# Ten inner chunks of two feed-forward layers are turned in 32 x 32 blocks on VectorE, and ScalarE's and VectorE's orders in the two input projections are changed

## The reference, cut to what matters

```
# block 1
h = rms_norm(x, mix_norm_g);  proj = h @ w_in          # 1024 -> 8708, then four kinds of attention
x = x + gated_mix(proj) @ w_out
h = rms_norm(x, mlp_norm_g)
x = x + square(relu(h @ w_up)) @ w_down                # inner width 4096
x = rms_norm(x, final_norm_g)
# block 2
h = rms_norm(x, norm1_g);     proj = h @ w_in2         # 1024 -> 2560: q, k, v and u
u -> (a, g);  c = a * sigmoid(g)                       # 512 channels
conv = silu(layer_norm(causal_conv31(c)))              # depthwise, 31 taps
x = x + concat(attention(q, k, v), conv) @ w_out2
h = rms_norm(x, norm2_g)
x = x + (silu(h @ w_gate) * (h @ w_up2)) @ w_down2     # inner width 2816
```

## Time and profile before

| | before |
|---|---|
| median of 3 runs | 799.73 us (799.54 to 800.09) |
| profiled execution | 797.38 us |
| its span, first to last instruction | 795.6 us |
| granted TensorE clock | 1.000 |
| busy: PE / PEld / DVE / ACT / POOL | 98% / 83% / 60% / 51% / 6% |

### The profile page before, as it was taken

One profiled execution on the slowest core, in us unless ns is written; L12 is line 12 of the kernel. 1 busy time (PEld: TensorE's weight loads), 2 busy tenths in 40 slices (PEclk: granted clock), 3 DMA queues, 4 the chain that ended last, 5 costly groups with the idle time before them and its releaser, 6 DMA issues.

```text
span 795.6 us, 9723 instructions
## 1 busy us (share of the span) xinstructions
PE 781.3 (98%) x3930; PEld 657.2 (83%) x3930; DVE 475.3 (60%) x623; ACT 406.9 (51%) x542; POOL 49.3 (6%) x38
## 2 busy tenths in 40 slices
PE   7999999999999999999999999999999999999998
PEld 5888899887888888888888887878988888888896
DVE  6654374764866877454444448699857554545443
ACT  6566365454656646555544455654565344343441
POOL 1000000000001410000000004022000000000000
PEclk9999999999999999999999999999999999999999
DMA  9843334433445366555656564845133755555341
GB/s 333 327 160 107 132 132 142 167 116 107 159 161 202 116 204 230 194 190 169 211 166 203 164 206 153 324 136 189 54 107 105 238 185 184 186 188 183 106 160 53
DMA packets 68508, 136.25 MB, mean 171 GB/s; under 512 B 2416, under 2 KB 7152, under 8 KB 67824
## 3 DMA queue, kind: packets, MB, share of 16 engines
q1 hardware_dynamic: 68320, 134.59, 49.7%
q10 hardware_dynamic: 144, 1.05, 0.4%
HBM read 134.43 MB, written 1.05 MB: 170 GB/s over the span
## 4 chain that ended last, share of the span: by engine, by line
PE 89%; DVE 7%; ACT 2%; DMA 1%; issue 1%; SPq 0%; ACTq 0%; DVEq 0%
PE b L592 19%; PE b L594 19%; PE b L593 19%; PE SS L592 4%; PE SS L594 4%; PE SS L593 4%; PE TT L561 4%; PE OO L592 2%; PE OO L594 2%; PE OO L593 2%; DVE wlo L1513 2%; DVE ca L1986 1%; PE b L737 1%; PE OO L911 1%; PE SS L680 1%; DMA raw<-in_w_in 1%
## 5 line engine op out<-in xcount | busy, mean ns | idle before, releaser
L1513 DVE TENSOR_TENSOR wlo<-raw,whi 128x2048 fp32r<-128x2048 f32 (+2 forms) x123 | 274.4, 2232 | 156.0 <-ACT whi L1081 155.8
L1081 ACT CAST whi<-raw 128x2048 fp32r<-128x2048 f32 (+2 forms) x123 | 227.5, 1851 | 126.3 <-PE b L594 83.3
L592 PE MATMUL b<-whi,Ahi 128*128 128x512 f32 (+2 forms) x552 | 216.4, 392 | 1.2 <-DVE Alo L1536 0.9
L594 PE MATMUL b<-whi,Alo 128*128 128x512 f32 (+2 forms) x552 | 209.2, 379 | 0.0
L593 PE MATMUL b<-wlo,Ahi 128*128 128x512 f32 (+2 forms) x552 | 208.7, 378 | 0.0
L592 PEld LDWEIGHTS b<-whi,Ahi 128*128 128x128 f32 x552 | 104.3, 189 | 20.4 <-DVE Alo L1536 1.7
L594 PEld LDWEIGHTS b<-whi,Alo 128*128 128x128 f32 x552 | 104.1, 189 | 20.1
L593 PEld LDWEIGHTS b<-wlo,Ahi 128*128 128x128 f32 x552 | 104.4, 189 | 17.5
L592 PE MATMUL b<-whi,Bhi 128*128 128x512 f32 x154 | 60.9, 395 | 0.0
L594 PE MATMUL b<-whi,Blo 128*128 128x512 f32 x154 | 60.0, 390 | 0.0
L593 PE MATMUL b<-wlo,Bhi 128*128 128x512 f32 x154 | 60.0, 390 | 0.0
(11 more groups left out here) (278 smaller groups left out, 1054.0 us busy)
## 6 DMA issues: line engine op xcount, KB each, us to landing
raw<-in_w_in SPq DMA_DIRECT2D x40, 1024.0 KB, 5.0
raw<-in_w_up SPq DMA_DIRECT2D x16, 1024.0 KB, 5.4
raw<-in_w_dn SPq DMA_DIRECT2D x16, 1024.0 KB, 4.9
raw<-in_w_d SPq DMA_DIRECT2D x11, 1024.0 KB, 4.9
raw<-in_w_g SPq DMA_DIRECT2D x10, 1024.0 KB, 4.9
raw<-in_w_u SPq DMA_DIRECT2D x10, 1024.0 KB, 5.1
raw<-in_w_out SPq DMA_DIRECT2D x8, 1024.0 KB, 4.9
raw<-in_w_br SPq DMA_DIRECT2D x4, 1024.0 KB, 4.9
```

Source lines behind the costliest of these rows:

```text
L592: e.matmul(dst, xh, H[:, kc, c0:ce], start=first and kc == krs[0], stop=False)
L594: ins = e.matmul(dst, xl, H[:, kc, c0:ce], start=False, stop=last and kc == krs[-1])
L1081: e.copy(whi[:, s, 0:m], raw[:, r, 0:m]).then_inc(s_hi, 1)
L1513: e.tensor_tensor(wlo[:, s, 0:m], raw[:, r, 0:m], whi[:, s, 0:m].bitcast(F32), ALU.subtract).then_inc(s_lo, 1)
```

## The change

**Turns.** The eight PE transposes of chunks 1 to 6 and 1 to 4 are gone. DVE turns the chunk instead, from `ust` to a new buffer `hT` in SBUF, in 16 instructions (`turn_part`): each takes 32 partitions x 256 elements and transposes its eight 32 x 32 blocks. Three quarters of them stand before the groups 1 to 3 of `dn j-1` (`d2 j-1`), the last quarter before the first group of the next chunk. ACT's `hhi` and DVE's `hlo` are made from `hT`, before the next chunk's second and third group.

**First projection, ACT.** `te` and `pc` (now `banks1`) and `evac` stand ahead of the split of each step, where they stood behind it.

**Second projection.** `ug` writes its second half of channels to `tg` with two instructions per token half in place of six; ACT (`ph`) copies it from there to `hp` and `odd` with six copies at steps 9 and 10. Two taps of the convolution move from step 12 to step 16.

```diff
-    bg[9] += [("ut", 1), ("ug", 1)]
+    bg[9] += [("ut", 1), ("ug", 1), ("ph", 0)]
+    bg[10] += [("ph", 1)]
-    for s, n in ((10, 7), (12, 2), (14, 3), (18, 2)):
+    for s, n in ((10, 7), (14, 3), (16, 2), (18, 2)):
         bg[s].append(("cv", n))
...
+        hT = sb("hT", [128, 2, 4, S], c=r4)
...
+    HV = {("H", j): i for i, j in enumerate(range(1, 7))}
+    HV.update({("G", j): 6 + i for i, j in enumerate(range(1, 5))})
...
-            if 0 < j < 7:
-                turn_h()
...
         for c in range(18):
             for q, (ui, t) in enumerate(order1(c)):
+                if q == 0 and c > 1:
+                    evac(c - 1, 1)
+                if q == 3 and c:
+                    evac(c, 0)
+                banks1(4 * c + q)
                 after("p1", c, ui, t)
...
-                if j == 1 and q == 1:
-                    hidden_hi(0)
+                if j and q == 1:
+                    hidden_hi(j - 1)
...
+        def ph(t):
+            w.wait_ge(s_ug, t + 1)
+            w.wait_ge(s_pad, 1)
+            u0 = 15 + 64 * t
+            for k in range(2):
+                u = tg[:, t, 128 * k:128 * k + 128].rearrange("p (u r) -> p r u", r=2)
+                for i, p in ((2 * k, 0), (2 * k + 1, 64)):
+                    e.copy(hp[p:p + 64, i, u0:u0 + 64], u[p:p + 64, 0, :])
+                ins = e.copy(odd[:, k, u0:u0 + 64], u[:, 1, :])
+            ins.then_inc(s_ph, 1)
...
+        def turn_part(key, m, landed_h):
+            k, j = key
+            w.wait_ge(*landed_h)
+            src = ust[:, j % 2, :, :].rearrange("p t (k c) -> p t k c", k=4)
+            dst = hT[:, j % 2, :, :].rearrange("p k (t q) -> p t k q", t=2)
+            for i in range(4):
+                ins = e.transpose(dst[32 * m:32 * m + 32, :, :, 32 * i:32 * i + 32],
+                                  src[32 * i:32 * i + 32, :, :, 32 * m:32 * m + 32])
+            if m == 3:
+                ins.then_inc(s_hv, 1)
...
+                if ("H", j - 1) in HV and q == 0:
+                    turn_part(("H", j - 1), 3, (s_up, 2 * j))
+                if j and q == 2:
+                    hidden_lo(j - 1)
...
+                    if ("H", j) in HV and k:
+                        turn_part(("H", j), k - 1, (s_up, 2 * j + 2))
...
-            u0 = 15 + 64 * t
-            for k in range(2):
-                a = src[:, 256 + 128 * k:384 + 128 * k].rearrange("p (u r) -> p r u", r=2)
-                g = ca[:, 2 + k, 128 * t:128 * t + 128].rearrange("p (u r) -> p r u", r=2)
-                bias = pcol("glu_b", 2 + k)
-                for i, p in ((2 * k, 0), (2 * k + 1, 64)):
-                    e.scalar_tensor_tensor(
-                        out=hp[p:p + 64, i, u0:u0 + 64], in0=a[p:p + 64, 0, :], scalar=bias[p:p + 64, :],
-                        in1=g[p:p + 64, 0, :], op0=ALU.add, op1=ALU.mult)
-                ins = e.scalar_tensor_tensor(out=odd[:, k, u0:u0 + 64], in0=a[:, 1, :], scalar=bias, in1=g[:, 1, :],
-                                             op0=ALU.add, op1=ALU.mult)
+            for k in range(2, 4):
+                ins = e.scalar_tensor_tensor(
+                    out=tg[:, t, 128 * k - 256:128 * k - 128], in0=src[:, 128 * k:128 * k + 128],
+                    scalar=pcol("glu_b", k), in1=ca[:, k, 128 * t:128 * t + 128], op0=ALU.add, op1=ALU.mult)
```

More of the change, by code:

```diff
@@ L262, in build @@
     s_tri, s_aw, s_ln, s_sg, s_u2 = sem("s_masks"), sem("s_a_write"), sem("s_lnsilu"), sem("s_silu"), sem("s_gateup")
+    s_ph = sem("s_phases")
     s_act = sem("s_act_step")
@@ L273, in build @@
         sem(n) for n in ("s_glu", "s_r4", "s_a_max", "s_a_recip", "s_convdve", "s_convfin", "s_lnnorm")]
+    s_hv = sem("s_hturn")
     s_dve = sem("s_dve_step")
@@ L398, in build @@
         X[key] = len(X)
-    XT = {key: i for i, key in enumerate(k for k in X if not (k[0] == "Y" and k[2]))}
+    HV = {("H", j): i for i, j in enumerate(range(1, 7))}
+    HV.update({("G", j): 6 + i for i, j in enumerate(range(1, 5))})
+    XT = {key: i for i, key in enumerate(k for k in X if not (k[0] == "Y" and k[2]) and k[:2] not in HV)}
     XG = {key: i for i, key in enumerate(k for k in X if k[0] in ("A", "N1", "N2", "N3"))}
@@ L479, in xplace, with turned, turned_half @@
         return hhi[:, a % 2], hlo[:, a % 2], 0, n, HC2[a]
+    def turned(key):
+        return (s_hv, HV[key[:2]] + 1) if key[:2] in HV else (s_xt, XT[key] + 1)
+    def turned_half(key):
+        k, j, t = key
+        return hT[:, j % 2, :, 128 * t:128 * t + 128]
     xbank = {}
@@ L533, in _ @@
             if i == unit_of["wo2", 0, 1, 0]:
-                w.wait_ge(s_pad, 1)
-                w.wait_ge(s_ug, 2)
+                w.wait_ge(s_ph, 2)
                 for k in range(2):
@@ L1206, in fl, with banks1 @@
             e.activation(e1, e1, ACT.Ln, bias=1.0).then_inc(s_fl, 1)
-        def stages1(s):
+        def banks1(s):
             for name, i in BG1[s]:
@@ L1211, in stages1 @@
                     te(i)
-                elif name == "sm":
+                elif name == "pc":
+                    pc(i)
+        def stages1(s):
+            for name, i in BG1[s]:
+                if name == "sm":
                     sm(i)
@@ L1227, in _ @@
             for q, (ui, t) in enumerate(order1(c)):
+                if q == 0 and c > 1:
[3 more added lines that the diff above has]
+                banks1(4 * c + q)
                 after("p1", c, ui, t)
[L1229 to L1232, removed]
+                if q == 0 and c == 1:
+                    evac(0, 1)
+                if q == 2 and c == 0:
+                    evac(0, 0)
                 stages1(4 * c + q)
@@ L1297, in relu2 @@
             if j >= 2:
-                w.wait_ge(s_xt, XT["H", j - 2, t] + 1)
+                w.wait_ge(*turned(("H", j - 2, t)))
             k = own(e.activation(o, bank[1 + t], ACT.Relu, scale=r2_[:, t:t + 1]))
@@ L1306, in hidden_hi @@
                     w.wait_ge(s_mm, done("dn", j - 2, 1, 1))
-                x_hi(("H", j, t))
+                if ("H", j) in HV:
+                    w.wait_ge(*turned(("H", j, t)))
+                    x_hi(("H", j, t), turned_half(("H", j, t)))
+                else:
+                    x_hi(("H", j, t))
         for j in range(8):
@@ L1406, in stages2 @@
                     gs(i)
+                elif name == "ph":
+                    ph(i)
                 elif name == "r0":
@@ L1471, in gated_hi @@
                     w.wait_ge(s_mm, done("d2", j - 2, 1, 1))
-                x_hi(("G", j, t))
+                if ("G", j) in HV:
+                    w.wait_ge(*turned(("G", j, t)))
+                    x_hi(("G", j, t), turned_half(("G", j, t)))
+                else:
+                    x_hi(("G", j, t))
         for j in range(6):
@@ L1479, in _ @@
                 after("g", j, ui, t)
-                if j == 1 and q == 1:
-                    gated_hi(0)
+                if j and q == 1:
+                    gated_hi(j - 1)
                 if q == 3:
@@ L2076, in _ @@
                 before("g", j, ui, t)
-                if j == 1 and q == 2:
-                    gated_lo(0)
+                if ("G", j - 1) in HV and q == 0:
+                    turn_part(("G", j - 1), 3, (s_u2, 2 * j))
+                if j and q == 2:
+                    gated_lo(j - 1)
                 if j == 0 and q == 0:
@@ L2090, in _ @@
                         gate_up(j, 1)
+                    if ("G", j) in HV and k:
+                        turn_part(("G", j), k - 1, (s_u2, 2 * j + 2))
                     if j == 5 and k == 3:
```

20 lines of the change are left out of this document (3 added, 17 removed).

## The result

| | before | after |
|---|---|---|
| median | 799.91 us (799.54 to 800.88, 4 runs) | 792.34 us (791.93 to 793.17, 4 runs) |
| ratio, 95% interval | | 0.9914 [0.9896, 0.9933] |
| profiled execution, its span | 797.38, 795.6 us | 793.17, 791.4 us |
| mean granted clock, profiled execution | 1.000 | 0.998 |

The account below looks back on a forecast made before the run. The prediction took PE, busy for 98% of the span, as the bound. Turns 8.7, first projection 1.0 and second projection 1.1 us sum to 10.8 off 799.73, so 788.9 us; range 786.5 to 793.0.

Parts of the forecast that it names:

- What bounds the kernel: Whole kernel: PE, busy 98% of the span; time taken off PE is gained if DVE and ACT keep their dates.
- the turns off PE: Feed-forward layers: ten chunks each lose eight PE transposes of 0.87 us in all, uncovered, a gain of 8.7 us.
- The turns on DVE: Feed-forward layers: 0.44 us per transpose, 7.0 us for 16, covered by DVE's waits up to 0.64 us each; cost 0.
- the date's zero: Block 1's feed-forward layer: the first down matmul of a chunk; `hlo` ready 18.6 us later, wanted by PE at 21.8.
- The first projection: ACT's copy ahead of the split lets PE go on 1.34 us earlier, less a new 0.35 us evacuation wait: 1.0 us gained.
- The lower bound of 0: First projection: no gain if splits waiting behind PE-gated copies come late once or twice elsewhere.
- The second projection: Rotary result 1.1 us earlier with ACT copies of 0.30 us; first PE wait gone, second 1.2 us; gain 1.1 us.
- the upper bound of 2.0: Second projection: the gain in us if ACT's small copies cost nothing.
- The sum: Whole kernel: 8.7 + 1.0 + 1.1 = 10.8 us off the median of 799.73, giving 788.9 us.
- rival A: Projections give nothing or lose up to 1.5 us through late splits or slow ACT copies: 791.0 to 792.5 us; chance 0.15.

Follow-up runs that it names:

- the turns alone: The kernel before with only the ten chunks turned on DVE, without the edits of either projection: 791.10 us, ratio 0.9883.
- the doubled transposes: The changed kernel with every DVE transpose issued twice, the first time into a scratch buffer: 812.05 us, ratio 1.0148 to the changed kernel.
- the evacuations alone ahead: The changed kernel with the first projection's evacuations ahead of the split, the copies behind it as before: 790.80 us, ratio 0.9891.
- the copies alone: The changed kernel with the first projection's copies ahead of the split in every step, the evacuations behind it as before: 790.96 us, ratio 0.9893.
- step 53 repaired: The changed kernel with ACT's old first-projection order, except step 53: copies ahead of the split, task 15's copy moved there from step 54: 786.33 us, ratio 0.9838.
- the same on the kernel before: The kernel before with only the edit of step 53 (copies ahead of the split, task 15's copy moved into it): 797.66 us, ratio 0.9964.
- the taps moved: The kernel with step 53 repaired, its two convolution taps moved on from step 16 to step 18: 786.67 us, ratio 0.9829 to before.
- one copy moved: The changed kernel with only task 15's copy moved from step 54 to step 53, ahead of the split: 789.20 us, ratio 0.9870.
- the first projection's old order: The changed kernel with ACT's order in the first projection as it was before: 788.87 us, ratio 0.9862.

## Why the prediction was right or wrong

**What bounds the kernel, and the turns off PE: right.** The period fell by 0.91 us where 0.87 was taken away, and the turns alone are worth 8.5 to 8.7 us (forecast 8.7).

**The turns on DVE: right, in its price and in its cover.** 0.436 us against 0.44 taken; the chunk's low part ready 18.6 us after the date's zero, as forecast. That the cover ends soon above is shown by the doubled transposes, with the six waits of the date. One thing was missing from it. For block 2's layer I counted DVE's date only; with slow transposes ACT's `hhi` would have been the first to be late, with the sigmoid behind it. At 0.44 us it costs nothing.

The Trainium skill, "VectorE: DVE Perf Modes", section "Rules for kernel authors", says to use TensorE for a 128 x 128 transpose if its result may go to PSUM. Here that rule decides wrongly. PE has no time to give away (98% busy) and DVE has; eight PE transposes cost 0.87 us of PE's time and sixteen on DVE 7.2 us (3.57 and 3.60) that nobody waits for.

**The first projection: wrong, and this is the step that failed.** "Late next is the second turn behind it, which wants DVE's `cb`, done at 196.74 + 0.49 = 197.23". The turn wants two things, the result of `cb` and an empty bank. The bank is emptied by ACT's next copy, and I had placed only the first copy ahead of the split; the order that I showed has the split between the two. So the wait of 1.94 us turned into one of 1.61. Shown by leaving that copy behind (nothing gained) and by moving it (the second turn then waits 0.28 us, for `cb`). The second half of the same term was also wrong: the split that now stood behind a PE-gated copy didn't only delay an evacuation; its low part on DVE went ahead of a `ys` that PE wanted (0.7 us), and evacuations ahead of splits made the turns of `ys` at 246 us late and then the first output group's low part (a wait of 0.8 us; both waits are there with the evacuations alone ahead and not with the copies alone). The lower bound of 0, for splits that "come late once or twice elsewhere", named this mechanism and put no price on it. Forecast 1.0 us of gain, measured 3.2 of loss: 4.2 us, which is more than the whole miss of 3.2. Of the 4.2, 1.3 is the gain that the bank held back. The rest is the places behind it, which cost 3.2 us where the forecast had 0.35 for one late evacuation; at most of them a low part on DVE comes late. The bank is shown by moving one copy. The later losses are shown as a whole, by the order taken out and put in alone, and are placed by the traces; no run repairs one of them by itself.

**The second projection: right mechanism, size off.** The copies take 0.24 us each, not 0.30, and the gain is 1.4 to 2.2 us by the runs instead of 1.1, at the upper bound of 2.0 rather than in the middle. The term that was too large is the price of the copies: the prediction had 1.1 us of gain at 0.30 us each and 2.0 at nothing, so cheaper copies make up a part of the difference; the rest isn't traced. The wait left is 0.61 us, not 1.2. The Trainium skill, "VectorE: DVE Perf Modes", section "The TRN2 errata", has 224 cycles and one per element at 1.2 GHz for ScalarE from SBUF, which gives an estimate of 0.24 us for 64 elements. The trace agrees, with 0.25 for one `odd` copy and 1.44 for six.

**The sum.** 8.7 (turns) + 2 (second projection) - 3.2 (first projection) = 7.5, against 7.6 measured. The time lies in the range, where rival A stood (791.0 to 792.5, chance 0.15), but not by A's account alone: late splits behind gated copies were there, no copy on ACT was slow, and the first projection's loss was larger than the 1.5 us that A allowed, with the second projection's gain against it. That the time still falls among A's is partly luck.

## What to carry to other kernels

When a wait is taken away, list everything that the next instruction needs, the buffer that it writes as well as its operands, and find each releaser's place in its engine's queue; the failing step had one operand and forgot the bank. A reorder is priced place by place: a long instruction that is put behind one gated by another engine can start late there, and so can what is queued behind its follower on the third engine. And before a whole order is changed, try the one step that the wait points to: with one step repaired the kernel took 786.33 us, with the order changed everywhere 792.34.

## What the runs showed of the hardware

**The granted clock fell behind waits of PE of 1.6 to 2.2 us, in some executions and not in others.** In the first projection a wait of 1.6 or 1.9 us stands among small matmuls at about 196 to 200 us. With it, the mean clock was 0.997 or 0.998 in 30 of 39 runs of before and in 24 of 40 of the other kernels that keep such a wait (the doubled transposes left out); without it, in none of 18 (step 53 repaired, the same on the kernel before, the taps moved, one copy moved). Where a profiled execution had the drop, 200 to 204 us read 0.57 or 0.58 (the changed kernel, the first projection's old order, the turns alone), with PE at 1.2 GHz for most of it, and with the copies alone ahead 202 to 204 us read 0.50; in the changed kernel PE had been busy for 0.55 of the 2.00 us before. The doubled transposes have the same drop in four more places, behind waits of 2.2, 2.2, 2.2 and 1.9 us, and none behind their waits of 1.4 us or less. The drop costs more time on top of the wait: with one copy moved PE gained 1.26 us of waiting and 1.58 us of low clock, 2.84 in all, and the medians fell by 3.1. The two levels of before stand 2.3 us apart, more than the 1.58; what the rest is isn't known. Nor is it known what lets the clock fall in one run and not in the next: the profiled execution of before had the 1.9 us wait and clock 1.000.

**A transpose on DVE of 32 partitions x 256 fp32 elements takes about the time of one pass over 256 elements**: 0.436 us, against 0.414 for the 128 x 256 form of the kernel before. Eight of them take 3.57 us, one every 0.45. Where each is issued twice from the same source, the second reads 0.394 us and a pair starts every 0.78 us.
